# Attention's weight cuts behind the bias, output bias on VectorE, first convolution tap on ScalarE, decay cuts one tile ahead

## What is computed

```python
# layer 0: banded attention (16 heads of 64, causal by chunks, relative bias), then an MLP
s = einsum('bqhd,bkhd->bhqk', q, k) * scale + bias
o = einsum('bhqk,bkhd->bqhd', softmax(s), v);  h = h + o @ w_o;  h = h + relu(rms(h) @ w1)**2 @ w2
# layer 1: recurrent block, then an MLP
u = rms(h) @ w_in + b_in
xc = conv_b + sum(xp[:, t:t + S] * conv_w[t] for t in range(4))      # four taps
a, i = gates(xc);  hs = scan(a, sqrt(1 - a * a) * (i * xc))
h = h + (hs * gelu(y_br)) @ w_o + b_o;  h = h + relu(rms(h) @ w1)**2 @ w2
# third part: gated linear attention (with decay), indexed attention, cross attention to mem; gated sum @ w_o
b = cumsum(log_sigmoid(a_low @ w_a_up + b_a) / 16)                    # per chunk of 64
q_d = q * exp(b);  k_d = k * exp(-b);  k_t = k * exp(b_last - b)
```

## Time and profile before

| | |
|---|---|
| median of 3 runs | 997.15 us (996.7 to 998.22) |
| the profiled execution | 997.31 us, its span 996.0 us |
| PE busy | 985.5 us |
| DVE busy | 686.0 us |
| ACT busy | 579.1 us |
| POOL busy | 80.2 us |
| HBM | 180 GB/s over the span |

### The profile page before, as it was taken

One profiled execution on the slowest core, in us unless ns is written; L12 is line 12 of the kernel. 1 busy time (PEld: TensorE's weight loads), 2 busy tenths in 40 slices (PEclk: granted clock), 3 DMA queues, 4 the chain that ended last, 5 costly groups with the idle time before them and its releaser, 6 DMA issues.

```text
span 996.0 us, 13520 instructions
## 1 busy us (share of the span) xinstructions
PE 985.5 (99%) x5222; PEld 835.8 (84%) x5222; DVE 686.0 (69%) x1157; ACT 579.1 (58%) x1008; POOL 80.2 (8%) x85
## 2 busy tenths in 40 slices
PE   9999999999999999999999999999999999999997
PEld 6887788888888997888888888887888888888886
DVE  6877686656668979766656678777777454677564
ACT  7677755444556796754445475557666544575443
POOL 3213110000004230000000000000120000000000
PEclk9999999999999999999999999999999999999999
DMA  9753455555554444455646556455444433335551
GB/s 370 287 199 127 170 174 206 194 208 176 205 176 169 164 169 169 170 199 182 226 176 208 175 209 227 169 188 192 173 143 150 169 127 127 127 127 194 187 190 42
DMA packets 27263, 180.32 MB, mean 181 GB/s; under 512 B 3008, under 2 KB 3904, under 8 KB 6464
## 3 DMA queue, kind: packets, MB, share of 16 engines
q1 hardware_dynamic: 26336, 176.89, 50.1%
q0 software_dynamic: 288, 2.10, 0.6%
q10 hardware_dynamic: 576, 0.47, 0.2%
HBM read 178.40 MB, written 1.05 MB: 180 GB/s over the span
## 4 chain that ended last, share of the span: by engine, by line
PE 84%; DVE 8%; ACT 5%; issue 2%; DVEq 0%; ACTq 0%
PE bank L323 23%; PE bank L281 13%; PE bank L283 13%; PE bank L282 13%; PE bank L331 12%; DVE lo L1281 3%; PE bank L296 1%; ACT L L885 1%; ACT hi L800 1%; DVE L L1354 1%; PE bank L448 1%; DVE L L1418 1%; PE bank L424 1%; PE bank L460 1%; PE bank L432 1%
## 5 line engine op out<-in xcount | busy, mean ns | idle before, releaser
L1281 DVE TENSOR_TENSOR lo<-raw,hi 128x1024 fp32r<-128x1024 f32 x318 | 383.9, 1253 | 23.0 <-ACT hi L800 22.8
L800 ACT ACTIVATE hi<-raw 128x1024 fp32r<-128x1024 f32 x318 | 320.0, 1050 | 85.1 <-PE bank L283 84.7
L323 PE MATMUL bank<-X,hi 128*128 128x512 f32 x1080 | 284.3, 395 | 0.0
L323 PEld LDWEIGHTS bank<-X,hi 128*128 128x128 f32 x1080 | 196.8, 189 | 34.8
L331 PEld LDWEIGHTS bank<-X,lo 128*128 128x128 f32 x1080 | 147.2, 190 | 10.8
L331 PE MATMUL bank<-X,lo 128*128 128x256 f32 x1080 | 150.5, 282 | 0.0
L831 ACT ACTIVATE bt<-bank 128x256 f32<-128x256 f32 x143 | 54.1, 380 | 153.5 <-PE bank L323 145.2
L1295 DVE TENSOR_TENSOR zr<-bank,bt 128x256 f32<-128x256 f32 x64 | 27.1, 424 | 108.9 <-ACT bt L831 108.9
L281 PE MATMUL bank<-hi,zh 128*128 128x512 f32 x256 | 100.0, 391 | 0.0
L283 PE MATMUL bank<-hi,zl 128*128 128x512 f32 x256 | 99.8, 390 | 0.0
L282 PE MATMUL bank<-lo,zh 128*128 128x512 f32 x256 | 99.7, 389 | 0.0
(11 more groups left out here) (308 smaller groups left out, 1399.5 us busy)
## 6 DMA issues: line engine op xcount, KB each, us to landing
raw<-in_w SPq DMA_DIRECT2D x64, 1024.0 KB, 4.8
raw<-in_rin SPq DMA_DIRECT2D x8, 1024.0 KB, 4.8
raw<-in_wk SPq DMA_DIRECT2D x4, 1024.0 KB, 8.7
raw<-in_wq SPq DMA_DIRECT2D x4, 1024.0 KB, 7.6
raw<-in_wo SPq DMA_DIRECT2D x4, 1024.0 KB, 4.8
raw<-in_mk SPq DMA_DIRECT2D x4, 1024.0 KB, 4.7
raw<-in_mv SPq DMA_DIRECT2D x4, 1024.0 KB, 4.7
raw<-in_rout SPq DMA_DIRECT2D x4, 1024.0 KB, 4.8
```

The source lines that it names most:

```text
L323: return PE.matmul(bank[b][:, :], wh[:, c:c + P], x[:, k_, :, :].rearrange("p a b -> p (a b)"), start=k_ == 0, stop=k_ == NC - 1, skip_gro ...
L800: ACTE.activation(hi[u_ % HIS][:, c], raw[u_ % RAW][:, c], ACT.Copy).then_inc(hi_cut, 1)
L1281: DVE.tensor_tensor(lo[u_ % RAW][:, c], raw[u_ % RAW][:, c], hi[u_ % HIS][:, c].bitcast(F32), ALU.subtract).then_inc(lo_cut, 1)
```

## The change

Four edits. (1) In the attention steps j = 0 to 7 DVE's cut moves from the start of a half step to between bias and normalisation, and `o_low` moves behind it; at j = 8 it stays. (2) POOL's addition of the output bias goes, and its four mk products move behind the eight of the gates; DVE adds the bias in two instructions of 128 x 1024, behind the cuts of rin 7. (3) ACT makes the first tap of each block, with scale and bias, behind both copies of a pair; DVE joins both blocks and then makes the three other taps of the two blocks by turns. (4) In the decay stage DVE cuts one tile further ahead before each sum.

```diff
@@ act(), to_x
                 second("rin", n, func=ACT.Identity, bias=gain("rec_b_in", n))
+            for n in (2 * i, 2 * i + 1):
+                a.wait_ge(*free["rin", n])
+                ACTE.activation(xc[:, n, :], xbr[:, n, 0:S], ACT.Identity, scale=gain("rec_conv_w", n),
+                                bias=gain("rec_conv_b", n)).then_inc(tap_made, 1)
@@ dve(), attention
-                at_half(name, t, e)
+                if j == 8:
+                    at_half(name, t, e)
                 if name == "wk":
                     joined(k[:, 2 * t + e, :], "wk", 2 * t + e)
                 if name == "wq":
                     joined(q[:, 2 * t + e, :], "wq", 2 * t + e, scale=0.125)
-                if e == 0 and j >= 2:
-                    o_low(j - 2)
                 if j < 8:
...
                     x.then_inc(free["s", i][0], 1)
-                    soft(i, TT)
+                    at_half(name, t, e)
+                if e == 0 and j >= 2:
+                    o_low(j - 2)
+                if j < 8:
+                    soft(2 * j + e, TT)
@@ dve(), to_x
                 joined(xbr[:, n, 3:XW], "rin", n)
-                d.wait_ge(*free["rin", n])
-                step(DVE.tensor_scalar(xc[:, n, :], xbr[:, n, 0:S], gain("rec_conv_w", n), gain("rec_conv_b", n), ALU.mult, ALU.add))
-                for w in range(1, 4):
-                    own()
+            for w in range(1, 4):
+                for n in (2 * i, 2 * i + 1):
+                    if w == 1:
+                        d.wait_ge(tap_made, n + 1)
+                        d.wait_ge(*free["rin", n])
+                    else:
+                        d.wait_ge(v_step, steps[0] - (0 if w == 3 and n % 2 else 1))
@@ dve(), recurrent block
+        lo_to(2 * (T_OF["rin", 5] + HIS))
+        d.wait_ge(bo_in, 16)
+        for s_ in range(2):
+            DVE.tensor_tensor(h[:, s_, :], h[:, s_, :], bo[:, :], ALU.add).then_inc(bo_added, 1)
         lo_to(2 * (T_OF["rin", 6] + HIS))
@@ dve(), decay
         for i in range(4):
-            at_tile("gv", i)
+            lo_to(2 * (T_OF["gv", i] + HIS))
             decay_sum(i)
             if i:
                 decayed(i - 1)
-        at_tile("dz", 0)
+        lo_to(2 * (T_OF["dz", 0] + HIS))
@@ pool()
-        g.wait_ge(bo_in, 16)
-        g.wait_ge(hn_made, 4)
-        g.wait_ge(ssq_made, 8)
-        POOL.tensor_tensor(h[:, :, :], h[:, :, :], bo[:, :].unsqueeze(1).to_broadcast([P, 2, D]), ALU.add).then_inc(bo_added, 1)
-        for j in range(2, 6):
-            by_rows(mk, "mk", j, "mem", 2, mk_scaled)
         for n in range(NC):
             g.wait_ge(*free["gate", n, 1])
             POOL.tensor_tensor(ig[:, n, :], ig[:, n, :], xc[:, n, :], ALU.mult).then_inc(gi_made, 1)
+        for j in range(2, 6):
+            by_rows(mk, "mk", j, "mem", 2, mk_scaled)
```

More of the change, by code:

```diff
@@ L117, in build @@
     z_made, z_high, z_low = sem("z_made"), sem("z_high"), sem("z_low")
-    xc_made, t_made = sem("xc_made"), sem("t_made")
+    tap_made, xc_made, t_made = sem("tap_made"), sem("xc_made"), sem("t_made")
     gi_made, a_made, aa_made, mass_made, root_made, drive_made = (
@@ L1431, in mlp @@
             else:
-                d.wait_ge(bo_added, 1)
+                d.wait_ge(bo_added, 2)
             add_rows(src_name)
@@ L1491, in to_x @@
                         step(x)
-                x.then_inc(xc_made, 1)
+                    else:
+                        x.then_inc(xc_made, 1)
         for i in range(4):
```

## The result

The changed kernel takes **1003.81 us** (median of 6 runs, 1003.4 to 1003.97), the kernel before 997.57 (6 runs beside it, 996.7 to 998.22): a ratio of 1.0063 with an interval of 1.005 to 1.0076. The forecast was 1000.6 with a range of 998.0 to 1002.6. So the sign was right and the size was not: +6.2 us where +3.5 was expected, and 1.2 us above the upper end of the range. The profiled execution took 1003.4 (span 1002.1, before 996.0).

A forecast was written before the change was run, and what follows sets the result against it. The prediction took TensorE (PE), busy 985.5 of 996.0 us, as the bound and counted its waits: attention +5.3, output bias -1.2, decay -0.6, in sum +3.5 us, so 1000.6 us as a median, range 998.0 to 1002.6.

The forecast's parts named there:

- The chain from s to s + 3.22: Attention: from the start of a half's last product (s), through join, bias and late cut, PE goes on at s + 3.22.
- before `wo`: At j = 6 PE waits 2.74 us for both halves of the first `wo` tile, 1.84 more than before.
- The five waits: Attention j = 1 to 5: PE waits 0.79 us at j = 1, then 0.55 in each step, restarts 0.10 each.
- With the tiles of `wo` (j from 6) no join is left, so there I count nothing: Attention steps from j = 6: later cuts there cost nothing, and a cut may come some tenths earlier.
- The clock falls: Rival: after the 2.74 us wait the next attention step runs at 1.2 GHz, +8, 1008.7 us; chance 0.02.
- the upper bound of attention, +8.1: Attention: each late cut begins just too late and waits for a whole GpSimd product, 2.8 us on top of +5.3.
- Output bias: Near 309 us: without GpSimd's 4.58 us addition a held cut ends earlier and two PE waits go, -1.2 us.
- Decay: Decay stage: cuts of gv 3 move ahead of the decay sums, removing PE's wait near 687 us, -0.63 us.
- Tap: First tap moved to ScalarE: VectorE gains on a path where PE shows no wait, so zero.
- the attention cuts are not late: Rival: no new attention waits come and the old 0.90 us wait goes, 994.4 us; chance 0.10.
- Half and half: Rival: attention at its low bound +4.0, and three further recurrent-stage waits go, -1.6, 997.8 us; chance 0.14.
- The gates come late: Rival: ScalarE's taps delay the sigmoids so PE waits for banks, 0.5 us per pair, 1002.6 us; chance 0.06.

The follow-up runs named there:

- Experiments 1: The kernel before with the attention edit alone: 1005.61 us, ratio 1.0079.
- 6: Changed kernel with the second half step's cut back ahead of the join, except at j = 5: 999.26 us, ratio 1.0019.
- 8: Changed kernel with only the second half step's cut at j = 5 put ahead of the join: 1001.09 us, ratio 1.0036.
- experiment 10: Changed kernel with GpSimd's product of k or q in second half steps waiting until VectorE's late cut is done: 1001.08 us, ratio 1.0036.
- Experiment 11: Changed kernel with the cuts of j = 6 and 7 back ahead of the bias: 1002.0 us, ratio 1.0047.
- experiment 9: Changed kernel with 11 unread PE products of 512 columns added ahead of the wait before `wo`: 1002.11 us, ratio 1.005.
- experiment 5: The kernel before with the first-tap edit alone: 997.75 us, ratio 1.0.

## Why the prediction was wrong in size and right in sign

- **The chain from s to s + 3.22** ended where it was forecast in the step that I read (j = 2 into 3), and 0.11 later before `wo` (92.92 - 89.59 = 3.33). The five waits with their restarts were put at 3.49 and measured 3.80; before `wo` 1.84 against 1.94. The misses are in the steps that were not read (j = 1 and 5, +0.13 and +0.15 each; why the chain is longer there is open). Experiments 1, 6 and 8 show these terms separately. GpSimd's share in the cut was put at 0.14 and is 0.21 (experiment 10).
- **"With the tiles of `wo` (j from 6) no join is left, so there I count nothing"** is the first step that failed: +1.36 us. The join was the reason I looked for, and it is not the only thing that can make a cut late. In these steps VectorE goes without a pause from the copy of `ol` over the normalisation (0.91 for the two blocks, beside a GpSimd product) and the bias to the cut. There was no slack for it: at the second tile PE wanted the half at 103.97, and the cut, 1.22 long, would have been late even from the start of the bias (102.89 + 1.22 = 104.11); at the third tile PE waited 0.27 even before the change. Experiment 11 shows it: with these cuts back in their place both waits vanish.
- **"The clock falls"** is the second: the mechanism was named, at the right place and for the right reason, but left out of the sum and given 0.02, because no wait of 0.9 us had done it. That was no evidence on one of 2.74, which, as the prediction itself said, is three times as long. The price was also wrong: a whole step at half clock (+8) where the trace has 3.4 us of it, 1.54 in the end. So the rival's time (1008.7) was far off as well; at +1.5 the case would have belonged to the upper end of the range. What the prediction cites of the Trainium skill (TensorE: Matmul & The Clock Gate, Part 1), that idleness brings the clock down, experiment 9 bears out. "By that rule it is this case" says more than that: of four traces with this wait the clock fell in three.
- With these two terms added to the forecast, 3.5 + 1.36 + 1.54 = 6.4, against 6.2 measured. Either alone would have left the time inside the range (1002.0 and 1002.1). The range was also narrower than its own terms: the upper bound of attention, +8.1, less the gains of 1.8, gives 1003.4, and was left out.
- **Output bias** -1.2: measured -1.33, in the change and alone. **Decay** -0.63: -0.76 in both, as the restart behind the wait goes with it. **Tap** 0: 0, and no wait on the sigmoids' banks came. GpSimd's mk products beside `mass` cost nothing that PE shows.
- Of the rivals, "the attention cuts are not late" fell with the five L331 waits. "Half and half" fell too: the three remaining L281 waits of the earlier trace rows, which it hoped to lose, do not show as jumps in the ledger; they stand at 382, 394 and 400 us (375, 387 and 393 before). "The gates come late" fell with experiment 5.

## What to carry to other kernels

Before work is moved behind a wait, look at what the moved piece feeds and count the chain from the event that ends the wait, at every iteration kind and not only at those where the new predecessor is the obvious one; a "nothing" in such a list needs its own row of slack. When one term of a forecast creates a long gap on TensorE, price the clock behind it as a part of that term, from a short stretch at half speed upwards, and check a window of a few microseconds, since a page of 40 slices doesn't show it. The idle time that an edit wants to fill can often be filled from ahead instead of from behind: here with both cuts in the half step that had the time (994.22 us), with one argument changed.

## What the runs showed of the hardware that I had not expected

- TensorE's granted clock fell from 2.4 to 1.2 GHz for 3.4 us behind a wait of 2.84 to 2.86 us in three traces (from 93.3, 93.9 and 89.8 us; the waits had ended at 92.92, 93.22 and 89.67, so 0.1 to 0.6 us earlier) and did not fall behind the same 2.84 us in a fourth (experiment 11), nor, by the mean clocks, in five of the ten runs of experiment 6. So the length of the wait alone does not decide. Behind 2.64 and 2.1 us it fell in none of five and four runs. What else decides was not tried. One thing differs between the traces: full clock began at 4.6, 5.1 and 4.5 us in the three with the fall and at 7.5 in the fourth (at 5.3 in experiment 9). It began at 5.9 and 6.0 in those with the shorter waits, so that even there it is not shown that the shorter wait alone saved the clock.
- 11 dummy products in such a wait (2.80 us of PE) made the kernel 1.7 us faster.
- A VectorE cut that starts beside a short GpSimd product lost 0.21 us (1.43 against 1.22), and since that stood at the end of a chain, each of six waits was longer by about this; with the clock behind it, it was 2.7 us in all.
- The first product behind a wait again costs 0.10 us more than the wait: jumps of 0.66 for waits of 0.56 (j = 2 to 4).
